# A hybrid decoder layer on one core: every SBUF tensor at 64 modulo 128 bytes

## The reference, cut to what matters

```python
xn = rms_norm(h, norm_mix_w); proj = xn @ w_in             # 1024 -> 3352 columns
ret_out = group_norm(retention(rope(rq), rope(rk), rv)) * silu(rg)      # 8 heads of 64
nsa_out = gated sum of compressed, selected and window attention        # 8 query heads, 2 kv heads
h = h + concat(ret_out, nsa_out) @ w_out                   # 1024 x 1024
hn = rms_norm(h, norm_ffn_w)
gate_pre, val = split(hn @ ffn_w_up, 2)                    # 1024 -> 2 x 2816
h = h + (silu(causal_conv3(gate_pre)) * val) @ ffn_w_down  # 2816 -> 1024
h = h + sigmoid(h @ ple_gate_w) * (p @ ple_w)              # 1024 x 1024, 256 x 1024
out = rms_norm(h, final_norm_w)
```

## Time and profile before

| | |
|---|---|
| median of three runs | 1704.76 us |
| the profiled execution, its own time | 1703.56 us |
| its span, first to last instruction | 1701.8 us |
| mean granted TensorE clock | 0.985 of full |
| TensorE matmuls (PE), busy | 1640.0 us, 96% |
| VectorE (DVE), ScalarE (ACT), GpSimd (POOL), busy | 1022.6, 626.8, 77.9 us |
| DMA, mean | 65 GB/s |

### The profile page before, as it was taken

How to read it: one execution, slowest core, us unless ns; L and a number is a source line. 1 busy time by engine, 2 the same in 40 slices (tenths; PEclk the granted TensorE clock), 3 DMA queues, 4 the chain that set the end, 5 groups by cost and what they waited for, 6 DMA issues and landing times.

```text
span 1701.8 us, 22018 instructions
## 1 busy us (share of the span) xinstructions
PE 1640.0 (96%) x8157; PEld 1328.3 (78%) x8157; DVE 1022.6 (60%) x1871; ACT 626.8 (37%) x1173; POOL 77.9 (5%) x126
## 2 busy tenths in 40 slices
PE   8899999998789999999999999999999999999997
PEld 6688888888666776678888888888888888888885
DVE  6833556555699988864346555555655565556432
ACT  6214434344677777752222211221221122114221
POOL 0111221121000000000000000000000000000000
PEclk9899999998799999999999999999999999999999
DMA  5433233226000000060111111211121111122000
GB/s 197 130 100 117 94 105 105 85 81 202 25 23 17 13 14 1 1 235 0 54 59 48 63 37 37 64 48 37 37 74 37 37 51 60 37 75 100 25 38 37
DMA packets 48987, 110.60 MB, mean 65 GB/s; under 512 B 8848, under 2 KB 17040, under 8 KB 48912
## 3 DMA queue, kind: packets, MB, share of 16 engines
q1 hardware_dynamic: 41488, 85.47, 15.1%
q0 software_dynamic: 7424, 24.12, 4.2%
HBM read 89.65 MB, written 19.92 MB: 64 GB/s over the span
## 4 chain that ended last, share of the span: by engine, by line
PE 87%; DVE 5%; ACT 2%; issue 2%; DVEq 0%; POOLq 0%; POOL 0%; ACTq 0%
PE ps L1461 27%; PE ps L1115 14%; PE ps L1117 14%; PE ps L1116 14%; PE ps L1261 4%; PE ps L1377 3%; PE ps L1334 2%; PE ps L1340 2%; PE ps L1448 1%; PE ps L1379 1%; PE ps L1284 1%; PE ps L1120 1%; PE ps L1380 1%; PE ps L1342 1%; DVE nb L1867 1%
## 5 line engine op out<-in xcount | busy, mean ns | idle before, releaser
L2005 DVE TENSOR_TENSOR h<-h,ps 128x512 f32<-128x512 f32 x336 | 225.3, 686 | 148.8 <-PE ps L1117 147.8
L1461 PE MATMUL ps<-htl,wuh 128*128 128x512 f32 x672 | 209.7, 393 | 0.0
L1461 PE MATMUL ps<-hth,wuh 128*128 128x512 f32 x672 | 209.6, 393 | 0.0
L1461 PE MATMUL ps<-hth,wul 128*128 128x512 f32 x672 | 209.6, 393 | 0.0
L1115 PE MATMUL ps<-wh,xth 128*128 128x512 f32 (+1 forms) x448 | 186.8, 417 | 14.8 <-DVE wl L1595 13.2
L1117 PE MATMUL ps<-wh,xtl 128*128 128x512 f32 (+1 forms) x448 | 170.9, 381 | 0.0
L1116 PE MATMUL ps<-wl,xth 128*128 128x512 f32 (+1 forms) x448 | 170.4, 380 | 0.0
L1059 ACT ACTIVATE ffh<-ffa 128x1024 fp32r<-128x1024 f32 x22 | 23.3, 1060 | 369.8 <-DVE ffa L2032 369.8
L1461 PEld LDWEIGHTS ps<-hth,wuh 128*128 128x128 f32 x672 | 126.3, 188 | 29.3
L1461 PEld LDWEIGHTS ps<-hth,wul 128*128 128x128 f32 x672 | 126.2, 188 | 29.1
L1461 PEld LDWEIGHTS ps<-htl,wuh 128*128 128x128 f32 x672 | 126.3, 188 | 28.8
(11 more groups left out here) (270 smaller groups left out, 3151.8 us busy)
## 6 DMA issues: line engine op xcount, KB each, us to landing
wuraw<-in_w_up SPq DMA_DIRECT2D x44, 512.0 KB, 5.1
wraw<-in_w_in SPq DMA_DIRECT2D x48, 256.0 KB, 3.3
proj_d<-stage POOLq DMA_DIRECT2D x48, 256.0 KB, 2.4
wdraw<-in_w_down SPq DMA_DIRECT2D x22, 512.0 KB, 3.6
rin<-proj_d POOLq DMA_DIRECT2D x32, 256.0 KB, 4.2
xraw<-in_xt SPq DMA_DIRECT2D x16, 256.0 KB, 5.8
owraw<-in_w_out SPq DMA_DIRECT2D x8, 512.0 KB, 5.6
h<-in_x SPq DMA_DIRECT2D x1, 4096.0 KB, 15.6
```

The source lines that it names most:

```text
L1461: mm = nc.tensor.matmul(ps[:, 2 * part + half, :], w_, x_[:, k, half * 512:(half + 1) * 512], start=(k == 0 and i == 0), stop=(k == NK - 1 ...
L2005: nc.vector.tensor_tensor(hh, hh, ps[:, 4 + o_ % 4, :], ALU.add).then_inc(dn_add, 1)
```

## The change

The rounding of each size goes from 32 to 128 bytes, and the first region starts 64 bytes later.

```diff
@@ class Region, def put
         t = self.nc.alloc_sbuf_tensor_at(name, shape, dt, offset=self.at)
-        self.at += (size + 31) // 32 * 32
+        self.at += (size + 127) // 128 * 128
         return t
@@ def build
-        base = Region(nc, 16512)
+        base = Region(nc, 16512 + 64)
```

## The result

The changed kernel takes 1686.51 us (median of 4 runs, 1685.26 to 1688.31) where the kernel before takes 1704.51 (4 runs, 1703.89 to 1705.28): ratio 0.9898, 95% interval 0.9887 to 0.9910. 1686.6 was forecast. The profiled execution took 1685.26 us, 18.30 less than the one before. The total came out as predicted. Of its four terms one did not come at all and another only in part; stretches of the trace that the forecast had put at 0, in which the clock differs between the two executions, made up for them.

The account below looks back on a forecast made before the run. TensorE's matmul count times spacing was taken to bound the kernel from 837 us on. Terms 14.9 + 0.6 + 1.6 + 1.1 = 18.2 us off the profiled 1703.56 gave 1685.4, the median 1.2 above: 1686.6 us, range 1681 to 1699.

Parts of the forecast that it names:

- Item 1: FFN tiles 1 to 20 with their down products: 2880 matmuls at 226.67 ns take 652.80 us, 14.9 us less.
- item 2: FFN tile 0: 96 matmuls at 6.6 ns less each, 0.6 us saved.
- B: Rival: interleaving up and down products costs a rhythm of its own; half the FFN gain stays out, 1694 us; chance 0.09.
- Item 3: After tile 21: down products 0.64, part products 0.32, gate's token tiles 2 and 5 0.64, together 1.6 us saved.
- Item 4: Retention inside the projection: some 180 waits of 234 ns shorten by 6 ns, 1.1 us saved, bounds 0 and 2.
- Item 5: Transposes by ident_f, moved from 0 to 64: 2 us lost or gained possible over 592 of prob, taken as 0.
- Item 6: VectorE and ScalarE, weight subtractions: no dependence on address, so 0.
- Item 7: DMA loads moved from 0 to 192 modulo 256: 0 taken, at most 2 us either way in the first 40 us.
- The rule of independent read ports: Skill page on TensorE's two read ports: position can't matter, time stays at 1704.8 us; the prediction disagreed with it.
- Rival C: Stationary operands are fast at 448 modulo 512; those moved to 192 turn slow, net +3.7, 1708.5 us; chance 0.06.
- D of the rivals: Half-clock stretches: a stage before 500 us beginning earlier can add or drop one, about 2 us either way; no chance given.

Follow-up runs that it names:

- m1: Changed kernel with moving operands left at 192 modulo 256, odd FFN tiles' weights put at 128, even tiles' and ffh, ffl at 64, gth2 at 192: 1702.82 us.
- m2: Changed kernel with the large region begun 64 bytes later: moving operands and even FFN tiles' weights at 0 modulo 256, odd tiles' weights at 192: 1691.26 us.
- v2: Kernel before with 192 bytes ahead of act_ and 224 ahead of gth2, FFN and last-stage stationary operands matching their moving ones modulo 256, retention left: 1686.98 us.
- e2_rest_only: Changed kernel with act_ and the FFN buffers put back to 0 modulo 256, all other tensors at their new places: 1702.92 us, ratio 0.9998.
- x_after: Changed kernel with one more 64-column matmul ahead of each down product in FFN tiles 1 to 20 (320 in all): those tiles take 696.51 us.
- e1_ffn_only: Kernel before with 192 bytes of padding ahead of act_, so only the FFN buffers and those in their places move to 192 modulo 256: 1688.12 us, ratio 0.9904.
- x_before: Kernel before with the same 320 small 64-column matmuls ahead of the down products in FFN tiles 1 to 20: those tiles take 701.34 us.
- m4: Changed kernel with stationary minus moving first byte, modulo 256, set to +96 (odd FFN tiles), -96 (even), -32 (down product, gth2): 1707.94 us.
- m6: Changed kernel with only wul1, the low part of the odd FFN tiles' weights, moved by 128 bytes to 64 modulo 256: 1695.67 us.
- m3: Changed kernel with the large region begun 128 bytes later: moving operands and even FFN tiles' weights at 64 modulo 256, odd tiles' weights and gth2 at 192: 1694.06 us.

## Why the prediction was right, and where it was not

**The bound.** Right. PE is never idle in the FFN, nothing else became late, and the spacing of the matmuls in the chain, not their busy time, is the quantity that changed.

**The reading of the spacing.** The step "stationary at 64 modulo 128 costs 226.7 ns, one at 0 or 96 costs 233.3, with the moving operand at 64" fits the rows that the prediction shows, but it is a special case: all moving operands of long runs but the part product's lay at 192 modulo 256, and so did all fast stationary ones. m1 shows that 64 modulo 128 is slow at D = 128, m2 that 0 is fast at D = 0. The change works because it puts nearly everything at 192 modulo 256. The reading also took each spacing as a matter of that matmul's own operands; the 1.39 us of the odd value halves and the part product's 230.0 ns came from their neighbours. Item 1 did not suffer by it, since it was worked out from the whole 667.73 us. The one exception, gth2 at 64 modulo 256, was named as the test, and it told.

**Item 1, item 2.** 14.93 us measured for 14.9, 0.57 for 0.6. The rival of a price for interleaving (B) was wrong for the changed kernel: with one D the up and down products keep 226.7 ns. With two D, as before, the mixing did cost: 230.8 ns for the odd tiles' up products in the value half.

**Item 3.** 1.09 us for 1.6. The down products gave 0.57 (0.64 forecast), the part products 0.27 (0.32), and the gate's token tiles 2 and 5 only 0.03 (0.64); v2, in which gth2 is at D = 0, gets 0.58 there. The gate's other token tiles, forecast at nothing, gave 0.20.

**Item 4.** The failed step. 1.1 us less was forecast, 0.46 more measured, and e2_rest_only has the same loss without the FFN's change. The row behind it, 234 ns ahead of a retention matmul, was put down to the weight load of an operand at 0. The load's address was not its cause: after the change the same place has 234 ns with all operands at D = 0. A run broken by small matmuls fits instead, since x_after makes 0.24 us ahead of a small matmul where there was none. The term took 1.1 between bounds of 0 and 2, and the measured loss lies outside both; why it is a loss is open.

**Item 5.** Taken at 0. A gain or loss by the identity's place does not show: from the 2700th matmul of the trace to the 4000th, in the attention, 227.35 us passed before, 227.23 after. The identity was not moved alone. The 3.3 ns from which the item took its 2 us either way were not a price of the moving operand's place: they came from the part product's 230.0 ns, and at D = 0 among neighbours at D = 0 that product has 226.7 (m2).

**Item 6.** 1219 and 1219 ns for the two subtractions, 1219 and 1220 before.

**Item 7.** wuraw lands in 5.1 us and wdraw in 3.6, as in the earlier trace rows, though wuraw now begins at 192. xraw's median went from 5.8 to 6.7 us, but that is scatter: in the traces with xraw at 0 modulo 256 it is 5.4 to 6.6 us (kernel before, e1_ffn_only, m2, v2, x_before), in those with it at 192 5.5 to 7.0 (changed kernel, e2_rest_only, m1, m4, m6, x_after). "DMA: Bandwidth & Descriptors" of the Trainium skill ("How a descriptor splits into AXI transactions") makes starts off a multiple of 256 bytes dearer; no landing time here shows that for the address in SBUF.

**The rule of independent read ports.** What the "SBUF — State Buffer" page of the Trainium skill ("Who interferes with whom") states would leave the time at 1704.8; the runs say that the distance of the two TensorE streams is worth up to 7.5 ns on 226.7. Whether they collide in the memory or elsewhere was not shown.

**Rival C** (448 modulo 512) is excluded by the changed kernel itself: wuh1 at 192 and wuh0 at 448 modulo 512 both run at 226.7.

**The clock (D of the rivals).** The profiled execution has no half-clock stretch at 485 us, and 1.45 us less from the 2250th to the 2700th matmul. e2_rest_only, m1, m3, m6 and x_after lack it too; the kernel before, e1_ffn_only, x_before, m2, m4 and v2 have it, and m4 has the attention's addresses of the changed kernel. So the address alone does not decide it; whether it has a share is open, since all four kernels with the old places of the rest have the stretch and only two of the eight others. The changed kernel also has 3.4 us less at half clock between 403 and 415 us. The forecast's closeness to 0.1 us is luck to that extent: the terms as measured make 16.1 us, not 18.2, and 2.2 us came from stretches put at 0.

## What to carry to other kernels

Where TensorE is never idle and the matmuls have 512 columns, read the spacing of starts by buffer, not the busy time: two buffers of one line with two spacings point to their addresses. Put the stationary and the moving operand of a long run at the same place modulo 256, the high and the low part both, and every run that is mixed with it; a layout rule for all tensors is not needed. Count only part of such a gain where small matmuls break the run every few products: a third of it was left here, 4.8 of 14.9 us.

## What was not expected of the hardware

- The spacing of 512-column fp32r matmuls in a long run goes by D: 226.7 ns at 0, wherever the two lie (0, 64 and 192 were tried), 228.8 to 228.9 at -64, 232.4 to 234.2 at the other distances in steps of 32.
- It belongs to the run, not to the single matmul alone: up products at D = 0 take 230.8 ns with down products at D = +64 between them (kernel before, odd tiles), and one weight load in three at D = 128 slows those at D = 0 beside it to 230.3 to 234.2 ns. After a break the first five at D = 0 need 230 ns each, and 128x64 matmuls in between cost 137 ns each, against 105 in the kernel before, where only the odd tiles' gate halves ran at 227 ns.
- With the retention operands moved from D = +64 to D = 0 against the projection, the mixed stage became 0.5 us longer and not shorter (258.57 and 258.58 us in the changed kernel and e2_rest_only against 258.11, 258.07 and 258.03 in the kernel before, e1_ffn_only and v2). ident_r and the constants moved with them, so the cause is open.
